# Decay sums and key scales spread by DMA from rows in memory in place of one spreading product per chunk

## The chip, the cores and the metric

The kernel runs on one core of a Trainium2 chip. The metric is the device time of one execution in microseconds (us), the median of the runs.

## The reference, cut to what matters

The model is two blocks, one after the other, on 256 tokens of width 1024. The first block has a gated delta rule beside a sparse attention and an MLP; the second has two layers with a dense and an eight-expert feed-forward part. The change lies in the delta rule. Of each head (8) and chunk, with `g` the log decays and `beta` the gates:

```python
    gc = jnp.cumsum(g, axis=-1)
    decay = jnp.exp(jnp.where(tri_incl, gc[..., :, None] - gc[..., None, :], -jnp.inf))
    kb = k * beta[..., None]
    A = jnp.where(tri_strict, jnp.einsum('bhncd,bhnsd->bhncs', kb, k) * decay, 0.0)
    ...
    w = jnp.einsum('bhncs,bhnsd->bhncd', Tm, kb * jnp.exp(gc)[..., None])
    attn = jnp.einsum('bhncd,bhnsd->bhncs', q, k) * decay
    q_dec = q * jnp.exp(gc)[..., None]
```

`k` and `q` are first scaled to length one, so a token's key carries a factor 1/length. The kernel uses chunks of 128 tokens, so with eight heads there are 16 matrices `m` of 128 by 128 (head `m // 2`, half `m % 2` of the 256 tokens), and a 17th that packs the 16 leading tokens of all eight heads.

## The kernel before

One program for each engine, written out in a fixed order; each waits on named events (semaphores). `q.wait_ge(...)` waits, `.then_inc(*q.did(...))` gives an event. SP only issues DMAs: `sp_blocks` walks a list of weight blocks of 1 MB (eight k-tiles by 256 columns) through a ring of six slots and waits before each until TensorE has used the block that was in its slot; between blocks it issues the other transfers at places named in `sp`. The blocks of the first stage are gk 0 to 3, gq 0 to 3, gv 0 to 3, gz 0 to 3. Each block is cast to a high half by ScalarE (`act_high`, L410) and a low half by VectorE (`dve_low`, L425), and TensorE makes three products of the halves for every tile (`mm3`, L435 to L437). A projected tile goes through a convolution: one tap on ScalarE (L901), three on VectorE (L923), then Silu on ScalarE (L910), then GpSimd squares it (L931) and TensorE sums the squares (L944).

PSUM has eight banks that `Banks.take` hands out in turn; whoever takes a bank waits until its last reader is done.

Beside this run the matrices of the delta rule. `gG` holds the log decays, a column for each matrix; `gB` the gates. `pe_gate_sums` makes the cumulative sums `GC` along the partitions (a column for each matrix). `pe_decays` makes the same sums along the columns, alike on all 128 partitions: a product for each matrix whose stationary operand is the column of `gG` broadcast to 128 columns. `act_factors` (L856) takes the exponential of that in groups of four matrices (it multiplies the queries later). `dve_decays` (L869) subtracts `GC` and cuts off at 0, `act_decays` (L861) takes the exponential in place, and `pool_decays` (L876, L878) multiplies with the two triangular masks into `AT` and `dec`. The five groups are 0 to 3, 4 to 7, 8 to 11, 12 to 15 and 16. ScalarE goes on with `act_l2`, the square root of the keys' lengths (L953); VectorE inverts it (L823) and makes `gBr`, gate over length. `pe_betas` spreads `gBr` over the partitions in the same way, and `dve_betas` (L890) multiplies it into `AT`; then `dve_keys` (L988, L992) takes the key products in, while ScalarE scales the keys (L983). The decays stand in the order of all engines behind block gq 0, the betas of groups 0 and 1 behind gq 2, of 2 and 3 behind gq 3, of the last behind gv 0. When all is in, VectorE inverts the small diagonal blocks (L1200) and spreads them (L1214), and TensorE turns them (L1221) and starts the large inverse. L1703 and L1374 belong to later work, L3500 stores the output, and L3469 reads two rows of gains over all partitions.

Of the kernel before, what the change touches and what calls it, by code (L numbers as in the profile page):

```python
# [15 lines left out]
P = 128  # L16
# [250 lines left out]
def emit(A, cst, out, sem, counts, off, arena, arena_r, ring, ring_r, hi_ring, C, vec, sm, posi, ix, flag, bank):  # L267
# [235 lines left out]
    wr = shaped(small(64), (8, 8))  # L503
    dtb, alog = small(8), small(8)
    eps6, eps5, one1, idle1 = small(1), small(1), small(1), small(1)
    bwr = shaped(sm[:, smtop[0]:smtop[0] + 64], (8, 8))
# [25 lines left out]
    smallT = at(23040, T)  # L532
    wsm, wsmall = at(6400, 8, 24), pair_at(6592, 8, 24)
    l2sq = [at(19456 + SEQ * j, SEQ) for j in range(8)]
    metasq = at(21504, P)
# [183 lines left out]
    def pool_load(q):  # L719
        q.e.memset(ss, 1.0).then_inc(*q.did())  # L720
        for ap, v in ((eps6, 1e-6), (eps5, 1e-5), (one1, 1.0)):
            q.e.memset(ap, v).then_inc(*q.did(("eps",)))
        q.wait_ge(("hi", "half", 1))
        q.e.tensor_tensor(first_half(1, ring_r), first_half(1, ring), first_half(1, hi_ring).bitcast(F32), ALU.subtract).then_inc(*q.did(("lo", "half", 1)))
        q.mark("load")
# [119 lines left out]

    def pe_decays(q, g):
        q.wait_ge(("gG",), ("gB",))
        ps = B.take(q, "decay", g[0])
        for x, m in enumerate(g):
            t = q.e.matmul(ps[:, x * P:(x + 1) * P], gG[:, m:m + 1].to_broadcast([P, P]), cc("Ub" if m == 16 else "U"), start=True, stop=True)  # L850
        t.then_inc(*q.did(("ps", "decay", g[0])))

    def act_factors(q, g):
        q.wait_ge(("ps", "decay", g[0]))
        q.wait_all("load")
        q.e.activation(flat(ebs[g[0] // 4]), B("decay", g[0]), ACT.Exp).then_inc(*q.did(("eb", g[0])))  # L856

# [5 lines left out]
    def dve_decays(q, g):  # L863
        ps = B("decay", g[0])
        q.wait_ge(("ps", "decay", g[0]), ("GC",))
        if g[0] != 16:
            q.wait_ge(("eb", g[0]))
        for x, m in enumerate(g):
            q.e.tensor_scalar(dec[:, m, :], ps[:, x * P:(x + 1) * P], GC[:, m:m + 1], 0.0, ALU.subtract, ALU.min).then_inc(*q.did(("dec0", g[0])))  # L869
        B.drop(("decay", g[0]), ("dec0", g[0]))  # L870

# [7 lines left out]

    def pe_betas(q, g):  # L880
        q.wait_ge(("gBr",))
        ps = B.take(q, "beta", g[0])
        for x, m in enumerate(g):
            t = q.e.matmul(ps[:, x * P:(x + 1) * P], gBr[:, m:m + 1].to_broadcast([P, P]), ident, start=True, stop=True)
        t.then_inc(*q.did(("ps", "beta", g[0])))

    def dve_betas(q, g):
        n = len(g) * P
        q.wait_ge(("ps", "beta", g[0]), ("AT0", g[0]))
        q.e.tensor_tensor(fl(AT, g), fl(AT, g), B("beta", g[0])[:, 0:n], ALU.mult).then_inc(*q.did(("AT1", g[0])))  # L890
        B.drop(("beta", g[0]), ("AT1", g[0]))

# [109 lines left out]
    def act_values(q, g):  # L1002
        q.wait_ge(("ps", "vT", g[0]), ("gB",))
        for x, m in enumerate(g):
            q.e.activation(vb[:, m, :], B("vT", g[0])[:, x * P:(x + 1) * P], ACT.Copy, scale=gB[:, m:m + 1]).then_inc(*q.did(("vb", g[0])))
        B.drop(("vT", g[0]), ("vb", g[0]))
# [25 lines left out]
    def pe_delta_in(q):  # L1032
        for i in range(1, 4):
            for j in pe_tiles(q, "gk", i, "gk", nX, 0, T, xn):
                if j == 2:
                    pe_gate_rows(q)
                if j == 6:
                    pe_gate_meta(q)
            if i >= 2:
                pe_l2(q, "gk", i - 2)  # L1040
        for i in range(4):
            for j in pe_tiles(q, "gq", i, "gq", nX, 0, T, xn):
                if j == 0:
                    pe_gate_sums(q)
            if i == 0:
                for g in groups:
                    pe_decays(q, g)
                pe_l2(q, "gk", 2)
            if i == 1:
                pe_l2(q, "gk", 3)  # L1050
            if i == 2:
                B.full("l2", "gk")
                for g in groups[0:2]:
                    pe_betas(q, g)
                    pe_keys(q, g)
                pe_l2(q, "gq", 0)
            if i == 3:
                pe_l2(q, "gq", 1)
                for g in groups[2:4]:
                    pe_betas(q, g)  # L1060
                    pe_keys(q, g)
        for i in range(4):
# [3 lines left out]
            if i == 0:  # L1066
                pe_betas(q, groups[4])
                pe_keys(q, groups[4])
# [7 lines left out]
    def act_delta_in(q):  # L1076
        for i in range(4):
            if i == 1:
                act_high(q, W.at["gk", 1] + 2)
                act_gate_rows(q)  # L1080
            act_channels(q, "gk", i)
        act_silu(q, "gk", 7)
        act_high(q, W.at["gq", 0] + 2)
        act_gate_sums(q)
        for i in range(4):
            act_channels(q, "gq", i)
            if i == 0:
# [2544 lines left out]
    def sp(e):  # L3632
        q = Engine(e, "sp", counts, sem)
        sp_first(q)
        for i in sp_blocks(q, W):
            if i == 2:
                sp_smalls(q)
            elif i == NRAW - 1:
                sp_consts(q)
# [56 lines left out]
```

## Time and profile before

| | |
|---|---|
| time, median of 3 runs | 1814.17 us (1813.74 to 1815.82) |
| profiled execution: time, span | 1815.71 us, 1814.0 us |
| busy in the span: TensorE, VectorE, ScalarE, GpSimd | 1790.4, 1394.8, 1075.1, 122.6 us |
| moved by DMA | 438.91 MB, 242 GB/s in the mean |

The busy times are sums over one profiled execution. The stage of the change lies between 36 and 143 us of the span. In the rows below PE is TensorE, DVE VectorE, ACT ScalarE, POOL GpSimd and SPq the queue of SP; times are counted from the start of the span. A number in brackets with an arrow is the idle time of the engine before the instruction and what ended it.

### The profile page before, as it was taken

The page shows a single profiled execution, that of the slowest core. Times are in us where ns is not written, and L with a number is a line of the kernel's source. Part 1 is how long each engine was busy: PE and PEld are TensorE (multiplying, and loading weights), DVE is VectorE, ACT ScalarE, POOL GpSimd, SP SyncE. Part 2 cuts the span into 40 slices and gives each one's busy share as a digit, 9 for nine tenths or more (in the row PEclk, how much of TensorE's full clock was granted, in tenths as well). Part 3 has the DMA queues.
Part 4 walks back from the last instruction along what each step waited for, and adds up shares of the span by engine and source line. Part 5 has one row for each costly group of instructions (what it writes and reads, how often), then busy time and mean ns, then how long its engine had stood idle before and what let it go on. Part 6 is the DMA issues. An engine that isn't in the chain of part 4 may idle for free.

```text
span 1814.0 us, 26895 instructions
## 1 busy us (share of the span) xinstructions
PE 1790.4 (99%) x11464; PEld 1611.7 (89%) x11464; DVE 1394.8 (77%) x1643; ACT 1075.1 (59%) x1198; POOL 122.6 (7%) x138
## 2 busy tenths in 40 slices
PE   9999999999999999999999999999999999999997
PEld 8999999999988999998998888888888888888885
DVE  6896487567674566655677899888889898889897
ACT  7753444556544444444336777767777776767674
POOL 1453150000000100000010000000000000000000
PEclk9999999999999999999999999999999999999999
DMA  9341333556555545565453599989998999899993
GB/s 287 116 129 48 94 117 117 181 183 217 186 187 198 186 151 185 185 231 168 152 173 118 202 379 373 369 315 374 352 376 309 377 349 378 308 379 349 378 368 134
DMA packets 260039, 438.91 MB, mean 242 GB/s; under 512 B 10341, under 2 KB 132792, under 8 KB 259784
## 3 DMA queue, kind: packets, MB, share of 16 engines
q1 hardware_dynamic: 259912, 437.11, 69.3%
q8 instruction: 92, 1.51, 0.3%
q14 instruction: 35, 0.29, 0.0%
HBM read 436.04 MB, written 1.05 MB: 241 GB/s over the span
## 4 chain that ended last, share of the span: by engine, by line
PE 90%; DVE 7%; ACT 2%; issue 1%; DMA 0%; SPq 0%; DVEq 0%; ACTq 0%
PE bank L437 26%; PE bank L435 26%; PE bank L436 26%; DVE ring_r L425 2%; PE bank L3208 1%; ACT hi_ring L410 1%; PE bank L3125 1%; PE bank L2488 1%; PE bank L1352 1%; PE bank L1344 1%; DVE arena L923 1%; PE bank L1811 1%; DVE arena L1714 0%; PE bank L1586 0%; DVE arena L1200 0%
## 5 line engine op out<-in xcount | busy, mean ns | idle before, releaser
L425 DVE TENSOR_TENSOR ring_r<-ring,hi_ring 128x2048 fp32r<-128x2048 f32 x402 | 906.9, 2282 | 248.3 <-ACT hi_ring L410 248.2
L410 ACT CAST hi_ring<-ring 128x2048 fp32r<-128x2048 f32 (+1 forms) x404 | 757.5, 1903 | 140.9 <-PE bank L437 140.6
L435 PE MATMUL bank<-hi_ring,arena_r 128*128 128x512 f32 (+1 forms) x1526 | 569.0, 373 | 0.7 <-DVE ring_r L425 0.7
L436 PE MATMUL bank<-ring_r,arena_r 128*128 128x512 f32 (+2 forms) x1534 | 567.4, 370 | 0.0
L437 PE MATMUL bank<-hi_ring,arena_r 128*128 128x512 f32 (+1 forms) x1526 | 566.4, 371 | 0.0
L435 PE MATMUL bank<-ring_r,hi_ring 128*128 128x256 f32 (+1 forms) x1400 | 400.1, 286 | 0.0
L437 PE MATMUL bank<-ring_r 128*128 128x256 f32 (+1 forms) x1400 | 395.4, 282 | 0.0
L436 PE MATMUL bank<-ring_r,hi_ring 128*128 128x256 f32 (+1 forms) x1400 | 395.3, 282 | 0.0
L435 PEld LDWEIGHTS bank<-hi_ring,arena_r 128*128 128x128 f32 x1526 | 286.8, 188 | 52.4 <-DVE ring_r L425 2.4
L436 PEld LDWEIGHTS bank<-ring_r,arena_r 128*128 128x128 f32 (+1 forms) x1534 | 287.9, 188 | 51.1
L437 PEld LDWEIGHTS bank<-hi_ring,arena_r 128*128 128x128 f32 x1526 | 286.9, 188 | 50.4
L435 PEld LDWEIGHTS bank<-ring_r,hi_ring 128*128 128x128 f32 x1400 | 264.6, 189 | 1.8 <-issue 1.0
L437 PEld LDWEIGHTS bank<-ring_r 128*128 128x128 f32 x1400 | 264.7, 189 | 0.0
L436 PEld LDWEIGHTS bank<-ring_r,hi_ring 128*128 128x128 f32 x1400 | 263.8, 188 | 0.2
L498 ACT CAST arena_r<-arena 128x256 fp32r<-128x256 f32 (+1 forms) x84 | 36.2, 434 | 80.1 <-DVE arena L2706 37.6
L498 ACT CAST arena_r<-bank 128x512 fp32r<-128x512 f32 (+1 forms) x62 | 32.3, 526 | 71.6 <-PE bank L3208 67.3
L3247 ACT ACTIVATE arena<-bank 128x512 f32<-128x512 f32 (+1 forms) x48 | 27.1, 564 | 64.6 <-PE bank L437 64.6
L494 DVE TENSOR_TENSOR arena_r<-arena,arena_r 128x256 fp32r<-128x256 f32 (+2 forms) x92 | 46.2, 507 | 3.2 <-ACT arena_r L498 2.2
L1653 ACT ACTIVATE arena<-bank 128x256 f32<-128x256 f32 (+1 forms) x27 | 10.4, 386 | 57.1 <-PE bank L437 57.1
L435 PE MATMUL bank<-arena_r,hi_ring 128*128 128x256 f32 x144 | 40.8, 283 | 0.0
L437 PE MATMUL bank<-arena_r,ring_r 128*128 128x256 f32 x144 | 40.7, 283 | 0.0
L436 PE MATMUL bank<-arena_r,hi_ring 128*128 128x256 f32 x144 | 40.4, 281 | 0.0
(422 smaller groups left out, 1641.8 us busy)
## 6 DMA issues: line engine op xcount, KB each, us to landing
ring<-in_w_gu_moe SPq DMA_DIRECT2D x176, 1024.0 KB, 6.3
ring<-in_w_down_moe SPq DMA_DIRECT2D x88, 1024.0 KB, 5.4
ring<-in_w_in SPq DMA_DIRECT2D x31, 1024.0 KB, 5.3
ring<-in_w_gu_dense SPq DMA_DIRECT2D x22, 1024.0 KB, 5.2
ring<-in_w_up SPq DMA_DIRECT2D x16, 1024.0 KB, 5.5
ring<-in_w_down SPq DMA_DIRECT2D x16, 1024.0 KB, 5.1
ring<-in_w_in_a SPq DMA_DIRECT2D x10, 1024.0 KB, 5.9
ring<-in_w_down_dense SPq DMA_DIRECT2D x10, 1024.0 KB, 5.1
```

The lines of the kernel that those rows point to most:

```text
L410: q.e.copy(hi_ring[:, b:b + m], ring[:, a:a + m]).then_inc(*q.did(("hi", of.tag, i)))
L425: q.e.tensor_tensor(ring_r[:, a:a + m], ring[:, a:a + m], hi_ring[:, b:b + m].bitcast(F32), ALU.subtract).then_inc(*q.did(("lo", of.tag, i)))
L435: q.e.matmul(ps, a[0], b[0], start=first, stop=False)
L436: q.e.matmul(ps, a[0], b[1], start=False, stop=False)
L437: return q.e.matmul(ps, a[1], b[0], start=False, stop=last)
L494: q.e.tensor_tensor(lo, src, hi.bitcast(F32), ALU.subtract).then_inc(*q.did(*done))
L498: q.e.copy(hi, src).then_inc(*q.did(*done))
L923: q.e.scalar_tensor_tensor(out=d, in0=ps[:, 0:T - u], scalar=vcol("conv_w", 24 * (3 - u) + w0 + j), in1=d, op0=ALU.mult, op1=ALU.add).then ...
L1344: t = q.e.matmul(ps[:, x * P:(x + 1) * P], MTs[i % 3][:, x, :], D[:, m, :], start=True, stop=True)
L1352: t = q.e.matmul(ps[:, x * P:(x + 1) * P], Ys[i % 3][:, x, :], DT[:, m, :], start=True, stop=True)
L1811: t = q.e.matmul(ps[p0:p0 + hd, qt * P:(qt + 1) * P], u["v"](j), pt[:, j, :], start=(x == 0), stop=(x == len(use) - 1))
L3247: q.e.activation(hh[:, c0:c0 + n], R.banks(R.tag, "up", x, j, 0)[:, 0:n], ACT.Silu).then_inc(*q.did(("hsilu", R.tag, x, j)))
```

## The change

The sums are made once as 17 rows: `pe_decay_rows` makes a product with `gG` as the stationary operand for 16 matrices and another for the 17th, ScalarE copies both from PSUM to SBUF, SP writes them to a new tensor `rows` in device memory and reads them back with a broadcast over all 128 partitions, group by group, into `dec`. `pe_beta_rows` transposes `gBr` in the middle of gq 2, and the same way leads into `betas`, which lies in the memory of `vb`. `act_factors` and `dve_decays` now read `dec` in SBUF; the latter is a `scalar_tensor_tensor` with a zero column, broadcast, as second input. `act_values`, which writes `vb`, waits for the group's `AT1`. The 34 spreading products and their ten bank turns are gone.

```diff
+    zero1 = small(1)
...
+    cumT, cum16T, betaT, betas = at(23400, P)[0:16, :], at(23528, P)[0:1, :], at(23656, P)[0:17, :], vb
...
-        for ap, v in ((eps6, 1e-6), (eps5, 1e-5), (one1, 1.0)):
+        for ap, v in ((zero1, 0.0), (eps6, 1e-6), (eps5, 1e-5), (one1, 1.0)):
...
-    def pe_decays(q, g):
-        q.wait_ge(("gG",), ("gB",))
-        ps = B.take(q, "decay", g[0])
-        for x, m in enumerate(g):
-            t = q.e.matmul(ps[:, x * P:(x + 1) * P], gG[:, m:m + 1].to_broadcast([P, P]), cc("Ub" if m == 16 else "U"), start=True, stop=True)
-        t.then_inc(*q.did(("ps", "decay", g[0])))
+    def row_of(a):
+        return a.rearrange("a (o b) -> o (a b)", o=1).to_broadcast([P, a.shape[0] * P])
+
+    def pe_decay_rows(q):
+        q.wait_ge(("gG",))
+        ps = B.take(q, "cumT")
+        q.e.matmul(ps[0:16, 0:P], gG[:, 0:16], cc("U"), start=True, stop=True)
+        q.e.matmul(ps[0:1, P:2 * P], gG[:, 16:17], cc("Ub"), start=True, stop=True).then_inc(*q.did(("ps", "cumT")))
+
+    def act_decay_rows(q):
+        q.wait_ge(("ps", "cumT"))
+        q.e.copy(cumT, B("cumT")[0:16, 0:P]).then_inc(*q.did())
+        q.e.copy(cum16T, B("cumT")[0:1, P:2 * P]).then_inc(*q.did(("cumT",)))
+        B.drop(("cumT",), ("cumT",))
+
+    def sp_decays(q):
+
+        q.wait_ge(("cumT",), ("end", "load", "pe"))
+        q.e.dma_start(A["rows"][0:16, :], cumT).then_inc(*q.landed("out_decay"))
+        q.e.dma_start(A["rows"][16:17, :], cum16T).then_inc(*q.landed("out_decay", ("out", "decay")))
+        q.wait_ge(("out", "decay"))
+        for g in groups:
+            q.e.dma_start(fl(dec, g), row_of(A["rows"][g[0]:g[-1] + 1, :])).then_inc(*q.landed(f"in_decay{g[0]}", ("in", "decay", g[0])))
 
     def act_factors(q, g):
-        q.wait_ge(("ps", "decay", g[0]))
+        q.wait_ge(("in", "decay", g[0]))
         q.wait_all("load")
-        q.e.activation(flat(ebs[g[0] // 4]), B("decay", g[0]), ACT.Exp).then_inc(*q.did(("eb", g[0])))
+        q.e.activation(flat(ebs[g[0] // 4]), fl(dec, g), ACT.Exp).then_inc(*q.did(("eb", g[0])))
...
     def dve_decays(q, g):
-        ps = B("decay", g[0])
-        q.wait_ge(("ps", "decay", g[0]), ("GC",))
+        q.wait_ge(("in", "decay", g[0]), ("GC",), ("eps",))
         if g[0] != 16:
             q.wait_ge(("eb", g[0]))
-        for x, m in enumerate(g):
-            q.e.tensor_scalar(dec[:, m, :], ps[:, x * P:(x + 1) * P], GC[:, m:m + 1], 0.0, ALU.subtract, ALU.min).then_inc(*q.did(("dec0", g[0])))
-        B.drop(("decay", g[0]), ("dec0", g[0]))
+        for m in g:
+            q.e.scalar_tensor_tensor(out=dec[:, m, :], in0=dec[:, m, :], scalar=GC[:, m:m + 1], in1=zero1.to_broadcast([P, P]), op0=ALU.subtract, op1=ALU.min).then_inc(*q.did(("dec0", g[0])))
...
-    def pe_betas(q, g):
+    def pe_beta_rows(q):
         q.wait_ge(("gBr",))
-        ps = B.take(q, "beta", g[0])
-        for x, m in enumerate(g):
-            t = q.e.matmul(ps[:, x * P:(x + 1) * P], gBr[:, m:m + 1].to_broadcast([P, P]), ident, start=True, stop=True)
-        t.then_inc(*q.did(("ps", "beta", g[0])))
+        ps = B.take(q, "betaT")
+        q.e.transpose(ps[0:17, 0:P], gBr, ident).then_inc(*q.did(("ps", "betaT")))
+
+    def act_beta_rows(q):
+        q.wait_ge(("ps", "betaT"))
+        q.e.copy(betaT, B("betaT")[0:17, 0:P]).then_inc(*q.did(("betaT",)))
+        B.drop(("betaT",), ("betaT",))
+
+    def sp_betas(q):
+
+        q.wait_ge(("betaT",))
+        q.e.dma_start(A["rows"][32:49, :], betaT).then_inc(*q.landed("out_beta", ("out", "beta")))
+        q.wait_ge(("out", "beta"))
+        for g in groups:
+            q.e.dma_start(fl(betas, g), row_of(A["rows"][32 + g[0]:33 + g[-1], :])).then_inc(*q.landed(f"in_beta{g[0]}", ("in", "beta", g[0])))
 
     def dve_betas(q, g):
-        n = len(g) * P
-        q.wait_ge(("ps", "beta", g[0]), ("AT0", g[0]))
-        q.e.tensor_tensor(fl(AT, g), fl(AT, g), B("beta", g[0])[:, 0:n], ALU.mult).then_inc(*q.did(("AT1", g[0])))
-        B.drop(("beta", g[0]), ("AT1", g[0]))
+        q.wait_ge(("in", "beta", g[0]), ("AT0", g[0]))
+        q.e.tensor_tensor(fl(AT, g), fl(AT, g), fl(betas, g), ALU.mult).then_inc(*q.did(("AT1", g[0])))
...
     def act_values(q, g):
-        q.wait_ge(("ps", "vT", g[0]), ("gB",))
+        q.wait_ge(("ps", "vT", g[0]), ("gB",), ("AT1", g[0]))
...
+            if i == 3:
+                pe_decay_rows(q)
             if i >= 2:
                 pe_l2(q, "gk", i - 2)
         for i in range(4):
             for j in pe_tiles(q, "gq", i, "gq", nX, 0, T, xn):
                 if j == 0:
                     pe_gate_sums(q)
+                if j == 4:
+                    pe_beta_rows(q)
             if i == 0:
-                for g in groups:
-                    pe_decays(q, g)
                 pe_l2(q, "gk", 2)
...
                 for g in groups[0:2]:
-                    pe_betas(q, g)
                     pe_keys(q, g)
...
             act_channels(q, "gk", i)
+        act_decay_rows(q)
         act_silu(q, "gk", 7)
...
         for i in range(4):
+            if i == 2:
+                act_beta_rows(q)
             act_channels(q, "gq", i)
...
+            elif i == W.at["gk", 3] + NRAW:
+                sp_decays(q)
+            elif i == W.at["gq", 1] + NRAW:
+                sp_betas(q)
```

The calls of `pe_betas` for groups 2, 3 and 4 go in the same way.

## Rows read from the trace of the kernel before

**Rows 1.** Busy time of each engine by stage; columns in its first line.
```profile
core 0: us, PE busy (x) PEld busy (x) DVE busy (x) ACT busy (x) POOL busy (x), PEclk, DMA share, GB/s
66.00:79.00 13.00, 13.00 (x109) 12.84 (x108) 12.44 (x30) 9.70 (x19) 8.20 (x9) 1.00 0.37 116
79.00:100.00 21.00, 21.00 (x177) 21.00 (x176) 20.02 (x43) 9.67 (x21) 6.02 (x6) 1.00 0.33 101
```

**Rows 2.** The chain that ended last: start us, us, what.
```profile
51.97 3.79 PE bank L850 x34
...
78.45 1.13 DVE arena L988 x4
...
142.50 1.26 PE bank L1221 x8
```

**Rows 3.** Timeline of VectorE: start us, us, engine, line, operation.
```profile
57.16 2.16 DVE L869 TENSOR_SCALAR arena<-bank,sm 128x128 f32<-128x128 f32 x8 [1.01 <-ACT arena L856]
59.55 2.42 DVE L869 TENSOR_SCALAR arena<-bank,sm 128x128 f32<-128x128 f32 x9 [0.23 <-ACT arena L856]
65.98 0.26 DVE L823 RECIPROCAL sm<-sm 128x17 f32<-128x17 f32 x1 [4.02 <-ACT sm L953]
...
74.69 0.68 DVE L890 TENSOR_TENSOR arena<-arena,bank 128x512 f32<-128x512 f32 x1
...
77.67 0.67 DVE L890 TENSOR_TENSOR arena<-arena,bank 128x512 f32<-128x512 f32 x1
```

**Rows 4.** Timeline of ScalarE, same columns.
```profile
48.64 0.43 ACT L910 ACTIVATE arena<-arena 128x272 f32<-128x272 f32 x1 [1.04 <-DVE arena L923]
...
56.45 1.09 ACT L856 ACTIVATE arena<-bank 128x512 f32<-128x512 f32 x2
...
62.48 1.88 ACT L410 CAST hi_ring<-ring 128x2048 fp32r<-128x2048 f32 x1
...
70.38 0.43 ACT L910 ACTIVATE arena<-arena 128x272 f32<-128x272 f32 x1 [1.93 <-DVE arena L923]
```

**Rows 5.** One line's instructions, L884: ns min/median/max.
```profile
L884 PE MATMUL bank<-consts,sm x34: 272/275/356, 69.7 to 93.7; 128*128 128x128 f32 x34
```

**Rows 6.** DMA issues (page), then lines L3500 (a store) and L3469 (a broadcast read).
```profile
ring<-in_w_in SPq DMA_DIRECT2D x31, 1024.0 KB, 5.3
...
L3500 SPq DMA_DIRECT2D out<-arena x4: 332/338/347, 1807.8 to 1811.3; - x4
...
DMA to landing us min/median/max: 2.0/2.3/2.7
...
L3469 SPq DMA_DIRECT2D arena<-in_vectors x2: 350/389/428, 1782.8 to 1783.2; - x2
...
DMA to landing us min/median/max: 3.5/4.2/5.0
```

**Rows 7.** GpSimd: line L876 as a whole, then its timeline.
```profile
L876 POOL TENSOR_TENSOR arena<-arena,consts x5: 469/1286/1305, 59.0 to 78.2; 128x512 f32<-128x512 f32 x4, 128x128 f32<-128x128 f32 x1
...
75.54 1.29 POOL L876 TENSOR_TENSOR arena<-arena,consts 128x512 f32<-128x512 f32 x1
...
80.21 0.61 POOL L931 TENSOR_TENSOR arena<-arena 128x256 f32<-128x256 f32 x1 [0.46 <-ACT arena L910]
...
86.47 2.13 POOL L931 TENSOR_TENSOR arena<-arena 128x256 f32<-128x256 f32 x1 [0.86 <-ACT arena L910]
```

**Rows 8.** Pairs of VectorE and GpSimd: timelines, then groups by line and form.
```profile
122.30 3.80 POOL L1374 TENSOR_TENSOR arena<-arena,consts 128x512 f32<-128x512 f32 x3 [1.76 <-PE bank L999]
...
123.85 1.03 DVE L1200 TENSOR_TENSOR arena<-arena 128x12 f32<-128x12 f32 x1
...
126.67 0.21 DVE L1200 TENSOR_TENSOR arena<-arena 128x30 f32<-128x30 f32 x1
...
L425 DVE TENSOR_TENSOR ring_r<-ring,hi_ring 128x2048 fp32r<-128x2048 f32 x399 | 903.2, 2290 | 237.1 <-ACT hi_ring L410 237.1
...
L1703 DVE SCALAR_TENSOR_TENSOR arena<-arena,sm 128x272 f32<-128x272 f32 x7 | 3.5, 502 | 3.4 <-ACT arena L1662 2.8
...
L1703 DVE SCALAR_TENSOR_TENSOR arena<-arena,sm 128x144 f32<-128x144 f32 x7 | 3.1, 440 | 0.7
```

More of the change, by code:

```diff
@@ L1059, in pe_delta_in @@
                 for g in groups[2:4]:
-                    pe_betas(q, g)
                     pe_keys(q, g)
@@ L1066, in pe_delta_in @@
             if i == 0:
-                pe_betas(q, groups[4])
                 pe_keys(q, groups[4])
@@ L3691 @@
     cst = nc.dram_tensor("in_table", table.shape, F32, kind="ExternalInput").ap()
+    aps["rows"] = nc.dram_tensor("rows", (64, P), F32).ap()
     out = nc.dram_tensor("out_0", (1, SEQ, 1024), F32, kind="ExternalOutput").ap()
```

## The prediction

> **What bounds the kernel now.** I read the page for the whole, then only the stretch that the change touches, 36 to 143 us: busy time by stage, the waits, the chain, and each engine's timeline. Every stage behind it starts on what this one delivers, so a shift at 142.5 us arrives at the end.
>
> In busy time by stage [rows 1] TensorE is full in every stretch, but so, nearly, is VectorE from 66 us on (12.44 of 13.00, 20.02 of 21.00). The chain [rows 2] runs through TensorE up to 78.45 us, the 3.79 us of the decay products among it, then through VectorE, and TensorE comes back into it only at 142.50, when VectorE releases it. I don't follow the chain before 78 us. VectorE's timeline [rows 3] has no gap at 78.45, its key product there simply follows on the beta product of 77.67. Its last real idle time is the 4.02 us that end at 65.98, and what ended it is ScalarE's square root [rows 3]. ScalarE in turn [rows 4] works without a break through the exponentials of the decays, the cast at 62.48, a table load behind it and the root. Those exponentials alternate with VectorE's 17 subtractions (57.16 to 61.97). So the path is: ScalarE and VectorE on the decays, cast, table load, root, then VectorE alone for 76 us. TensorE runs ahead of it and never holds it. TensorE's own slack at the end of the stretch is small (it waits a little before 142.50), but everything the change takes from TensorE adds to that slack.
>
> **The change, part by part.**
>
> TensorE. The 17 decay products are 34 passes of 3.79 us in all [rows 2]; the 17 beta products are 34 passes of the same kind (median 275 ns each, started about 0.11 us apart as 3.79/34) [rows 5], so 3.8 us. Added are two products (4 passes) and one transpose (1 or 2): 0.6 us. Net 7.0 us less. Worth 0 on the path, since VectorE from 66 us and ScalarE before it don't wait for these products. What hides TensorE's loss hides its gain as well. A new wait comes with it: the beta transpose stands inside the product of gq tiles 4 and 5, and needs gBr, which VectorE makes right behind 65.98. TensorE, 3.3 us early by then, waits there until about 66.6. That gives back what the decays saved; tile 5 is then done at about the time of before, and nobody waits for it.
>
> Decay rows: are they there in time? ScalarE copies the sums in the idle time before the activation of 48.64 (1.04 us idle) [rows 4], two copies of about 0.2 us; ready at 48.1. SP sends them out (two DMAs, 0.4 us apart), behind a weight block that is issued when gk 3 is done, at about 44, and lands in some 5.3 us [rows 6], so by 49.5. A store of 256 KB lands in 2.0 to 2.7 us [rows 6]: out at about 51.1. A broadcast read of 512 KB over the 128 partitions lands in 3.5 us when it is first [rows 6], the 256 KB store in 2.3; I take 2.8 for a group of 256 KB: first group at 53.9, the others about 0.7 us apart, the last at 56.8. Needed: first at 56.45, the last of the four behind 59.5. Worth 0, with 2.5 us of cover. Were the landing 5 us, it would be a stall of 1 to 2 us. Behind it in SP's queue stand weight blocks that come 1.5 us late, with six blocks loaded ahead: 0.
>
> Decay subtraction. Before: tensor_scalar with its input in PSUM, 17 in two runs of 2.16 and 2.42 us, 0.26 us apart [rows 3]. After: scalar_tensor_tensor with the broadcast rows in SBUF and a broadcast zero in SBUF. By itself it costs the same 0.26. But now it has two inputs in SBUF, and GpSimd's mask products of 1.29 us, two for each group, start at 59.0 [rows 7]; four in a row reach to 64.3, beside the second half of the subtractions. What the trace shows of such pairs [rows 8]: while GpSimd does its three products of 122.30 to 126.10, a VectorE product of 12 columns out of SBUF takes 1.03 us, ending as GpSimd's instruction ends; with GpSimd idle one of 30 columns takes 0.21. The scalar_tensor_tensor L1703 with 144 columns averages 440 ns against 502 for 272 columns; 128 columns fewer, at the 1.12 ns each of the low halves (2290 ns over 2048 columns), should leave 360, so some of the seven were held too. The other way, GpSimd's 0.61 us square took 2.13 us beside VectorE's subtraction for a low half (L425), at 86.47 [rows 7]. The PSUM forms at 59.55 ran beside GpSimd's product undisturbed [rows 3, 7].
>
> The Trainium skill says the same and more widely, on the page "SBUF — State Buffer", section "Who interferes with whom": a VectorE instruction with two SBUF inputs contends with a GpSimd instruction that reads SBUF, and whoever starts first holds the shared pair for the whole instruction. It counts inputs, not columns, so by it the one-column zero would count as the second input, a case that no row shows; by it the sum below stands, and without it (a one-column input taken as none) this term would be 0.
>
> Worked out: groups 0 and 1 (8 subtractions) are over at 59.3, before GpSimd holds anything. Group 2 starts at 59.55. GpSimd has five instructions before it next waits for ScalarE: four of 1.25 us and one of 0.6. VectorE gets one subtraction in behind each: 60.5, 61.9, 63.2, 64.6 (group 2 done), 65.4, then freely 65.6, 65.9, 66.1 (group 3) and 66.4. Before, the last ended at 61.97. ScalarE's last exponential, cast, load and root follow: +4.4 us at VectorE's 65.98. Bounds: 0 if a one-column input takes no port; at least 0.9 if VectorE waits only once (59.55 to 60.45); at most 5.3 if all 5.6 us of GpSimd's work lies ahead of VectorE's nine.
>
> Betas: late. All times here without the shift just found, which moves both sides alike. ScalarE copies the rows behind the activation of 70.38 [rows 4]: ready at 71.0. Out 2.0 to 2.7 [rows 6], issue and wait 0.05, back 2.3 to 3.5: the first group is there between 75.35 and 77.25, at my 2.3 and 2.8 at 76.15. VectorE wants it at 74.69 [rows 3]: a stall of 0.7 to 2.6, taken as 1.5 us, with all of VectorE's queue behind it (keys, the next low half, the convolutions of gq 3). Nothing hides it: group 0's mask product, the other input, is done by 60.4, and the beta products used to stand in PSUM by then. The later groups come in time.
>
> Beta products: 0.68 us for 512 columns out of PSUM and SBUF [rows 3]; out of SBUF alone 0.57 by the 1.12 ns a column of the low halves, and a start, so I take the same. But they too now have two SBUF inputs, and GpSimd's masks of groups 2 to 4 run up to about 79 [rows 7]. At 76.2 the instruction of 75.54 still has 0.6 us to go; the second product meets a short one, 0.3; the third the square of 86.47 that ends at 88.6, 0.5. Together 1.4 us; bounds 0 and 2.5 (two long ones whole).
>
> Sum on the path: 0 (TensorE) + 4.4 + 1.5 + 1.4 = 7.3 us. The profiled execution's span is 1814.0 and its time 1815.7, 1.5 us above the median of the three runs, 1814.17; a shift carries over to that median: 1821.5 us.
>
> **The rivals.** (1) TensorE is the bound after all, as the chain before 78 us says: then 7.0 us less, 1807.2. It decides if VectorE, in truth, follows TensorE's tiles between 66 and 142 us; against it stands that VectorE's busy time leaves under 1 us in 21 [rows 1], and that its waits name ScalarE [rows 3]. (2) The one-column zero takes no port; only the late betas and their port cost: 1.5 + 1.4 = 2.9 us, or 0.7 with the early landing and no collision: 1814.9 to 1817.1, no change that can be measured (a measurement of this kernel can tell about 0.2%, 3.6 us). (3) A transfer takes 5 us or more from issue to landing, as blocks do: decays 1 to 2 us late and betas 4 more, on top of the sum: 1825 and above. (4) Everything lands in time and nothing collides, 1814.
>
> **How the numbers follow.** Forecast (port and late betas) 0.60; rival (2) 0.18; (4) 0.07; (1) 0.08; (3) 0.07. The low bound of the first case is 0.9 + 0.7 = 1.6 us, its high bound 5.3 + 2.6 + 2.5 = 10.4 us. The range 1814 to 1825 holds the first two cases and most of (4); out are (1) and (3). Slower by over 0.2%: the first case but for its lowest part, and (3): 0.65. Within: 0.25. Faster: 0.10.
>
> **What would show it.** Right: VectorE's subtractions of groups 2 and 3 take over 1 us each with their ends on the ends of GpSimd's masks, the root comes near 70.4, the first beta product starts behind its DMA's landing, TensorE idles in front of the beta transpose, and TensorE's restart of 142.50 comes 7 us later. Wrong: subtractions that keep 0.26 us apart (then rival 2), a beta product without a wait, or a restart before 142.5 (rival 1).

## The result, and the profile after

The changed kernel takes 1823.64 us (1820.93 to 1824.82, 5 runs) against 1814.17 us (1813.74 to 1815.82, 5 runs): a ratio of 1.0045 by all the runs (the two medians alone would give 1.0052), 95% interval 1.0035 to 1.0056. The interval does not hold 1, so the changed kernel is slower, by about half a percent. The profiled execution of it took 1823.64 us, with a span of 1821.7 us, 7.7 us over the span of before.

Read first busy time by stage, beside [rows 1]:

```profile
core 0: us, PE busy (x) PEld busy (x) DVE busy (x) ACT busy (x) POOL busy (x), PEclk, DMA share, GB/s
66.00:79.00 13.00, 8.42 (x52) 8.42 (x53) 8.51 (x18) 9.88 (x16) 4.30 (x5) 0.62 0.10 22
79.00:100.00 21.00, 18.84 (x154) 18.45 (x153) 19.50 (x43) 11.15 (x26) 9.49 (x10) 1.00 0.59 191
```

From 66 to 79 us TensorE and VectorE both lost more than 3 us of work: TensorE stands idle, and its granted clock over the stretch is 0.62 of full speed, so much of it is spent at the lower level, 1.2 GHz. The DMA queues are nearly still (0.10 against 0.37). Something in front of this stretch is late. VectorE's timeline names it, beside [rows 3] (the single rows from 59.32 on come from narrow windows; they are the first five of the nine subtractions):

```profile
56.90 2.19 DVE L887 SCALAR_TENSOR_TENSOR arena<-arena,sm 128x128 f32<-128x128 f32 x8 [1.04 <-ACT arena L875]
59.32 6.72 DVE L887 SCALAR_TENSOR_TENSOR arena<-arena,sm 128x128 f32<-128x128 f32 x9 [0.23 <-ACT arena L875]
...
59.32 1.04 DVE L887 SCALAR_TENSOR_TENSOR arena<-arena,sm 128x128 f32<-128x128 f32 x1 [0.23 <-ACT arena L875]
60.29 1.44 DVE L887 SCALAR_TENSOR_TENSOR arena<-arena,sm 128x128 f32<-128x128 f32 x1
61.65 1.38 DVE L887 SCALAR_TENSOR_TENSOR arena<-arena,sm 128x128 f32<-128x128 f32 x1
62.95 1.42 DVE L887 SCALAR_TENSOR_TENSOR arena<-arena,sm 128x128 f32<-128x128 f32 x1
64.30 0.70 DVE L887 SCALAR_TENSOR_TENSOR arena<-arena,sm 128x128 f32<-128x128 f32 x1
...
70.05 0.26 DVE L825 RECIPROCAL sm<-sm 128x17 f32<-128x17 f32 x1 [4.01 <-ACT sm L979]
...
79.95 1.48 DVE L917 TENSOR_TENSOR arena<-arena 128x512 f32<-128x512 f32 x1 [1.11 <-DMA arena<-rows]
...
83.60 1.06 DVE L917 TENSOR_TENSOR arena<-arena 128x512 f32<-128x512 f32 x1
...
94.19 1.10 DVE L917 TENSOR_TENSOR arena<-arena 128x512 f32<-128x512 f32 x1
...
105.49 0.28 DVE L917 TENSOR_TENSOR arena<-arena 128x128 f32<-128x128 f32 x1
```

GpSimd's timeline beside it:

```profile
58.78 1.44 POOL L893 TENSOR_TENSOR arena<-arena,consts 128x512 f32<-128x512 f32 x1 [8.37 <-ACT arena L880]
60.30 1.29 POOL L895 TENSOR_TENSOR arena<-arena,consts 128x512 f32<-128x512 f32 x1
61.54 1.34 POOL L893 TENSOR_TENSOR arena<-arena,consts 128x512 f32<-128x512 f32 x1
62.96 1.27 POOL L895 TENSOR_TENSOR arena<-arena,consts 128x512 f32<-128x512 f32 x1
64.19 0.66 POOL L957 TENSOR_TENSOR arena<-arena 128x256 f32<-128x256 f32 x1
```

The first eight subtractions follow each other at 0.26 us, as before. Of the nine, five take 1.04, 1.44, 1.38, 1.42 and 0.70 us, and each ends within 0.2 us of the end of one of GpSimd's five instructions (60.22, 61.59, 62.88, 64.23, 64.85). Behind 64.85 the last four pass in 1.1 us. ScalarE waits for them, beside [rows 4], and SP's queue carries the betas' round trip, beside [rows 6]:

```profile
64.41 0.63 ACT L880 ACTIVATE arena<-arena 128x512 f32<-128x512 f32 x1 [4.14 <-DVE arena L887]
...
66.55 1.88 ACT L410 CAST hi_ring<-ring 128x2048 fp32r<-128x2048 f32 x1
...
74.78 0.24 ACT L904 COPY arena<-bank 17x128 f32<-17x128 f32 x1
```

```profile
50.97 2.24 SPq L870 DMA_DIRECT2D arena<-rows  x5
...
75.05 0.25 SPq L910 DMA_DIRECT2D rows<-arena  x1
76.59 2.24 SPq L913 DMA_DIRECT2D arena<-rows  x5
```

The chain that ended last, beside [rows 2], passes through both transfers, as it never did before:

```profile
61.65 4.14 DVE arena L887 x6
...
75.05 1.53 DMA rows<-arena
76.59 3.33 DMA arena<-rows
79.95 1.49 DVE arena L917
...
149.88 1.26 PE bank L1249 x8
```

TensorE's wait list has the expected new entry, `PEld bank L900 <- DVE sm L827: 7.3, 1, 7.3`: one wait of 7.3 us before the beta transpose. It restarts on the diagonal blocks, which it turns, at 149.88 instead of 142.50 [rows 2], 7.4 us later. This restart is called the restart below.

### The profile page after: what moved, and what is told of

Same layout as the page of the kernel before. It is cut to its first block, busy times and chain, and to the rows that moved or that the text cites. A ratio compares the mean times of both kernels' runs of the same rounds, so it can differ in the third digit from the quotient of the medians.

```text
span 1821.7 us, 26786 instructions
## 1 busy us (share of the span) xinstructions
PE 1789.5 (98%) x11401; PEld 1610.9 (88%) x11401; DVE 1400.7 (77%) x1643; ACT 1075.4 (59%) x1201; POOL 120.4 (7%) x139
## 4 chain that ended last, share of the span: by engine, by line
PE 88%; DVE 8%; ACT 3%; issue 1%; DMA 1%; SPq 0%; DVEq 0%; ACTq 0%
PE bank L437 26%; PE bank L435 26%; PE bank L436 26%; DVE ring_r L425 2%; DVE arena L949 1%; ACT hi_ring L410 1%; PE bank L3236 1%; PE bank L3153 1%; PE bank L2516 1%; PE bank L1380 1%; PE bank L1372 1%; PE bank L1614 1%; PE bank L1839 1%; DVE arena L1228 0%; PE bank L3360 0%
```

## The experiments

The delay is built up in four segments of one path, and each run is read by them (a beta product is VectorE's multiplication of the betas into `AT` for one group): from the first subtraction to the reciprocal, from there to the start of the first beta product, from there to the start of the last, and from there to TensorE's restart. In the kernel before they are 8.82, 8.71, 24.22 and 43.59 us: 57.16, 65.98, 74.69 and 142.50 [rows 2, 3], with

```profile
98.91 0.28 DVE L890 TENSOR_TENSOR arena<-arena,bank 128x128 f32<-128x128 f32 x1
```

The table gives what each kernel's single profiled execution adds to them, in us, and the ratio of all its runs (5 to 11) to those of the kernel before beside it (24 to 28 runs, median 1815.3 to 1815.7; for the first row the 5 runs given above, median 1814.17). The sum leaves out when the first subtraction starts: at 56.6 to 57.6 us in most executions, at 59.0 in that of masks_as_before and at 55.9 in the last two rows.

| kernel | subtractions to reciprocal | to first beta product | to last | to restart | sum | median | ratio (95%) |
|---|---|---|---|---|---|---|---|
| the change | 4.33 | 1.19 | 1.32 | 0.80 | 7.64 | 1823.64 | 1.0045 (1.0035-1.0056) |
| change_again | 4.33 | 1.08 | 1.46 | 0 | 6.86 | 1821.09 | 1.0034 (1.0021-1.0048) |
| decays_only | 4.38 | 0 | 0 | 0 | 4.35 | 1819.63 | 1.0023 (1.0013-1.0033) |
| scales_only | 0 | 1.02 | 1.52 | 0 | 2.53 | 1819.14 | 1.0018 (1.0009-1.0027) |
| zero_in_psum | 0 | 0.98 | 1.53 | -0.1 | 2.40 | 1816.83 | 1.0010 (1.0001-1.0019) |
| masks_wait | 0.08 | 2.55 | 1.37 | 0.4 | 4.44 | 1819.97 | 1.0023 (1.0012-1.0033) |
| filler | 4.36 | 1.14 | 1.41 | 0 | 6.94 | 1821.17 | 1.0034 (1.0021-1.0048) |
| copy_early | 4.33 | 0 | 1.11 | 0.5 | 5.94 | 1821.88 | 1.0032 (1.0020-1.0045) |
| repaired | 0 | 1.47 | 0.41 | 1.0 | 2.95 | 1817.99 | 1.0014 (1.0005-1.0023) |
| gpsimd_scales | 0 | 1.46 | -1.7 for both | | -0.20 | 1814.51 | 0.9995 (0.9986-1.0004) |
| masks_as_before | 0 | 0 | 0.2 for both | | 0.18 | 1816.22 | 1.0003 (0.9994-1.0012) |
| silu_later | 0 | 1.45 | -2.4 for both | | -0.87 | 1814.29 | 0.9994 (0.9985-1.0003) |
| before_silu_later | 0 | 0 | 0.3 for both | | 0.26 | 1815.35 | 1.0000 (0.9991-1.0009) |

**The change again (change_again).** The same kernel, timed beside the next three.

> The changed kernel once more, on the chip of the three runs beside it. The path's own delay in its profile is 7.4 us (TensorE's restart at 149.88 against 142.50), the medians are 9.5 us apart. If the 2 us between the two are only the spread of the executions of both kernels, this run lies 7 to 9 us above the kernel before; if they belong to the change (say, a lower clock of TensorE later on), 9 to 10 us again.

Slower again, by 5.8 us in the medians, which is less than the 7 to 9 us expected. The first three segments repeat to 0.15 us; the 0.80 us in the last one do not. They lay in VectorE's inversion, where in the first profile a 128-column product took 1.24 us beside GpSimd, and 0.29 in this one. Of the runs below four show nothing in that segment and three show 0.4 to 1.0 us: in copy_early the same product takes 1.24 us again, in masks_wait and repaired a product of 4 columns takes 1.09 and 1.19 instead of 0.66 in the kernel before. I take it for a chance of where GpSimd's three products of 1.3 us fall there; no run was made to show it.

**One half alone (decays_only, scales_only).** In the first the betas are spread by TensorE again, in the second the decays:

```diff
 # decays_only
-        q.e.tensor_tensor(fl(AT, g), fl(AT, g), fl(betas, g), ALU.mult)
+        q.e.tensor_tensor(fl(AT, g), fl(AT, g), B("beta", g[0])[:, 0:n], ALU.mult)
 # scales_only
-            q.e.scalar_tensor_tensor(out=dec[:, m, :], in0=dec[:, m, :], scalar=GC[:, m:m + 1], in1=zero1.to_broadcast([P, P]), ...)
+            q.e.tensor_scalar(dec[:, m, :], ps[:, x * P:(x + 1) * P], GC[:, m:m + 1], 0.0, ...)
```

> Only the decay sums go by way of memory; the key scales are spread by TensorE as before. Theory (second SBUF input of VectorE's subtraction collides with GpSimd's masks): the root comes at 69.8 as in the change, plus 4.1 us in all, 4 to 5 us above the kernel before. Rival A (the late key scales are the real cost and the subtractions' delay is swallowed later): within 1 us of the kernel before. Rival B (TensorE's idle time in front of the beta transpose lowers its clock and that costs): under 4 us, since that idle time is gone.

> Only the key scales go by way of memory; the decay sums are spread by TensorE as before, into PSUM. Theory: VectorE's subtractions keep 0.26 us apart and the root stays at 65.7; the first product of the scales waits about 1.2 us for its DMA, and three of the products take 0.4 to 0.8 us longer beside GpSimd: 2.5 to 3.5 us above the kernel before. Rival A (late scales are the real cost): 6 us or more.

The two parts add up: 4.35 and 2.53 make 6.88, and the whole has 6.86. VectorE's timeline of decays_only, then that of scales_only:

```profile
59.02 6.77 DVE L887 SCALAR_TENSOR_TENSOR arena<-arena,sm 128x128 f32<-128x128 f32 x9 [0.23 <-ACT arena L875]
...
78.50 0.68 DVE L925 TENSOR_TENSOR arena<-arena,bank 128x512 f32<-128x512 f32 x1
```

```profile
59.16 2.42 DVE L895 TENSOR_SCALAR arena<-bank,sm 128x128 f32<-128x128 f32 x9 [0.22 <-ACT arena L882]
...
75.33 1.67 DVE L926 TENSOR_TENSOR arena<-arena 128x512 f32<-128x512 f32 x1 [0.94 <-DMA arena<-rows]
```

The stretched subtractions come with the decays' half alone, the wait for the transfer and the long beta products with the betas' half alone. The time of scales_only, 3.9 us over the kernel before in the medians, is more than its 2.5 us on the path and more than the 3.5 expected. What the clock does to a time (below) is as large as the rest: the profiled execution, at a mean granted clock of 0.996, took 1816.53 us, the four at 0.993 took 1819.1 to 1820.6.

**The zero moved to PSUM (zero_in_psum).** The instruction, its counts and its first input stay; only the one column that holds the zero lies in a free column of a PSUM bank.

```diff
+        zp = B("cumT")[:, 256:257]
+        if g[0] == 0:
+            q.e.memset(zp, 0.0).then_inc(*q.did(("zp",)))
-   in1=zero1.to_broadcast([P, P])
+   in1=zp.to_broadcast([P, P])
```

> The whole change, but the zero column of the subtraction lies in PSUM, so that it has one SBUF input. Theory: the 17 subtractions are 0.26 us apart again, ScalarE's root comes near 65.7 in place of 69.7, and the time falls by 4 to 4.5 us against the change (some 3 to 4 us above the kernel before). Rival (the form scalar_tensor_tensor in place on DMA-written rows is slow, or ScalarE waits for the DMAs): no change against the changed kernel.

```profile
59.46 2.42 DVE L892 SCALAR_TENSOR_TENSOR arena<-arena,sm,bank 128x128 f32<-128x128 f32 x9 [0.25 <-ACT arena L875]
65.91 0.26 DVE L825 RECIPROCAL sm<-sm 128x17 f32<-128x17 f32 x1 [4.02 <-ACT sm L984]
...
75.59 1.71 DVE L922 TENSOR_TENSOR arena<-arena 128x512 f32<-128x512 f32 x1 [0.90 <-DMA arena<-rows]
```

6.72 us become 2.42, with GpSimd's masks of 58.92 to 64.2 us beside them as before. So a second input of one column, repeated for all 128, is enough for the collision when it lies in SBUF, and the whole first segment was this. What is left of the change, 2.40 us, is that of scales_only. The median, 1816.83 us, is 4.3 us under that of change_again, as expected, but only 1.5 us over the kernel before, where 3 to 4 were expected.

**GpSimd made to wait (masks_wait).** The zero is in SBUF again, but GpSimd starts its masks only when all subtractions are done (`if g[0] == 0: q.wait_ge(("dec0", 16))` in `pool_decays`).

> The whole change, and one wait more: GpSimd holds its first mask product until VectorE's 17th subtraction is done. Nothing else is touched; both SBUF inputs stay. Theory (the subtractions are slow only beside GpSimd's reads): they are 0.26 us apart, the last ends near 61.8, the root comes near 65.8, GpSimd starts some 3 us later, which nobody on the path notices: 4 to 4.5 us less than the change, 1 to 3 us above the kernel before. Rival (form, in-place access or the DMA-written rows make them slow): the subtractions stay at 1.3 us each and the added wait makes it slower by up to 3 us.

VectorE's timeline, and under it GpSimd's:

```profile
59.67 2.45 DVE L887 SCALAR_TENSOR_TENSOR arena<-arena,sm 128x128 f32<-128x128 f32 x9 [0.23 <-ACT arena L875]
66.14 0.26 DVE L825 RECIPROCAL sm<-sm 128x17 f32<-128x17 f32 x1 [4.02 <-ACT sm L981]
66.44 1.08 DVE L827 TENSOR_TENSOR sm<-sm 128x17 f32<-128x17 f32 x1
...
67.55 0.56 DVE L831 SCALAR_TENSOR_TENSOR sm<-sm 128x17 f32<-128x17 f32 x1
...
77.40 1.43 DVE L919 TENSOR_TENSOR arena<-arena 128x512 f32<-128x512 f32 x1 [1.18 <-DMA arena<-rows]
```

```profile
62.27 1.31 POOL L895 TENSOR_TENSOR arena<-arena,consts 128x512 f32<-128x512 f32 x1 [11.52 <-DVE arena L887]
...
66.23 1.26 POOL L897 TENSOR_TENSOR arena<-arena,consts 128x512 f32<-128x512 f32 x1
```

With GpSimd out of the way the subtractions are 0.26 us apart with both inputs in SBUF, so it is the pairing that costs and not the instruction. But the masks now lie 3.5 us later, beside the 17-column products L827 and L831 (0.18 us each otherwise), which are held for 1.08 and 0.56 us. That makes everything behind late by 1.3 us, the betas' rows with it, and the wait for them is still there: 4.3 us won, 1.5 of them given back. The expectation, that nobody on the path would notice GpSimd's late start, was wrong, and the median is 1.1 us under that of change_again instead of 4 to 4.5.

**TensorE kept busy (filler).** 30 products of the identity, written to unused columns, fill TensorE's wait in front of the beta transpose.

> The whole change, and 30 products of the identity with itself (60 passes, about 6.6 us) in TensorE's idle time in front of the beta transpose. If the lowered clock of TensorE behind that idle time (0.62 in the stage 66 to 79 us) costs time, this is 1 to 2 us faster than the change and its granted clock stays at full speed there. If TensorE has slack there, the time is that of the change within 1 us, at 5.5 to 6.5 us above the kernel before.

Windows 66 to 79 us of change_again, then of filler:

```profile
66.00:79.00 13.00, 8.27 (x60) 8.27 (x61) 8.67 (x18) 9.82 (x16) 4.14 (x5) 0.74 0.08 20
```

```profile
66.00:79.00 13.00, 12.51 (x107) 12.24 (x106) 8.68 (x19) 9.78 (x16) 4.06 (x5) 1.00 0.04 15
```

The granted clock rises from 0.74 to 1.00, and the restart stays (6.94 against 6.86 us). The idle TensorE and its low clock in this stretch cost nothing; they are a sign of the delay and not its cause.

**The betas' rows copied earlier (copy_early).** ScalarE's copy out of PSUM moves from the end of block gq 1, behind the tap of tile 3, to the middle of that block, behind the tap of tile 2.

```diff
+            if (name, j) == ("gq", 2):
+                act_beta_rows(q)
...
-            if i == 2:
-                act_beta_rows(q)
```

> The changed kernel with one thing moved: ScalarE copies the betas' rows out of PSUM right behind its tap and SiLU beside the third channel row of gq, where it had done so some us later, so their round trip through memory starts earlier. Theory (lateness and port add up): the first beta product no longer waits for its transfer (1.1 us in the changed kernel, and some 0.15 more for VectorE's issue), the subtractions stay at 6.7 us and the beta products at 1.1 to 1.6 us; restart of TensorE's chain at 148 to 149, time 1 us under the changed kernel, 1820 to 1822.5. Rival (the wait for the transfer is the whole cost of the beta part): the restart falls by 2.5 us or more. Rival (the copy then holds ScalarE's SiLU, which was due first): the restart doesn't move or goes up.

On the path it did as forecast: from the reciprocal to the first beta product it is 8.71 us again, without a wait, and the second segment's 1.1 us are gone. The time does not show it: 1821.88 against 1821.09 us for the change. The clock alone moves a time by more than 1 us from one execution to the next (below), so 1 us cannot be told here from the times, only from the path.

**What would repair it (repaired, gpsimd_scales, masks_as_before).** The first has the zero in PSUM, the early copy, and GpSimd's masks of all five groups before its squares of gq, so that the later beta products meet no mask. The second lets GpSimd do the beta products of groups 1 to 4 itself, in front of its squares of gq from tile 4 on. The third is the second with the old order of masks and squares. The diff is cut to GpSimd's order in the first two; its last two lines are not in repaired.

```diff
-        for g in groups[0:2]:
+        for g in groups:
             pool_decays(q, g)
         pool_l2(q, "gq", range(0, 4))
-        for g in groups[2:5]:
-            pool_decays(q, g)
...
+        for g in groups[1:5]:
+            pool_betas(q, g)
```

> The whole change with all three costs taken out: zero column in PSUM; ScalarE's copy of the key scales moved ahead by two tiles' work (from behind gq tile 3 to behind gq tile 2), so that they land before VectorE wants them; GpSimd's masks all ahead of its squares of the queries, so that none runs beside the products of the scales. Theory: root near 65.9, first product of the scales without a wait near 74.6 at 0.7 us, TensorE's restart near 142.5, the time within 1 us of the kernel before: the 7 us taken from TensorE are still worth nothing. Rival (TensorE's work counts once the waits are gone): 1 to 7 us faster than the kernel before.

> As repaired, and the products of the scales of groups 1 to 4 go from VectorE to GpSimd, which can read them now that they lie in SBUF (it cannot take part while they are in PSUM in this kernel's order). Theory (VectorE is the path from 66 to 142 us): it saves VectorE 3 times 0.78 and once 0.76 us, restart near 139.5 to 140.5, 2 to 3 us faster than the kernel before. Rival (the products then come late, or GpSimd's reads hold VectorE up by as much): within 1 us of repaired.

> The version with the zero in PSUM, the early copy of the betas' rows and GpSimd doing the last four beta products, but with GpSimd's masks and squares in the order of the changed kernel (masks of the first two groups, squares of gq, masks of the other three). If the two small VectorE operations beside the masks (0.59 and 1.23 us in that version, 0.18 for the second in the kernel before) are what costs it, this one restarts TensorE's chain 1 to 1.5 us earlier, at 141 to 141.6 where that version had 142.6, and takes 1813 to 1814.5. If the masks of the last groups are then late for the key products and the beta products that follow, the restart is at 143 or later and the time 1815 or more.

repaired was expected to be back within 1 us of the kernel before. It is 2.95 us late on the path and 2.6 us in the medians. Its timeline of VectorE:

```profile
66.42 0.59 DVE L827 TENSOR_TENSOR sm<-sm 128x17 f32<-128x17 f32 x1
66.93 0.16 DVE L829 TENSOR_TENSOR sm<-sm 128x17 f32<-128x17 f32 x1
67.04 1.23 DVE L831 SCALAR_TENSOR_TENSOR sm<-sm 128x17 f32<-128x17 f32 x1
...
76.29 0.68 DVE L922 TENSOR_TENSOR arena<-arena 128x512 f32<-128x512 f32 x1
```

The first beta product is free of wait and collision (0.68 us). But GpSimd's run of masks now stretches over the small products, which cost 1.46 us more. Moving the masks moved the collision. gpsimd_scales has the same 1.46 us and takes four of the five beta products off VectorE; the one left to VectorE takes 1.62 us instead of 0.68, now beside GpSimd's own beta products (four in 4.67 us from 75.00). It comes out level with the kernel before (ratio 0.9995), not 2 to 3 us faster as expected. In masks_as_before the small products are at 0.18 us again, as its expectation had it, but the time is not better. Its restart, at 144.53, proves less than it seems to: this execution was 1.8 us late before its first subtraction (59.00 against 57.16), and by the segments it is only 0.2 us behind the kernel before. VectorE, then GpSimd:

```profile
79.19 1.11 DVE L1031 TENSOR_SCALAR arena<-bank,sm 128x128 f32<-128x128 f32 x4
82.85 1.13 DVE L1027 SCALAR_TENSOR_TENSOR arena<-bank,sm,arena 128x128 f32<-128x128 f32 x4 [2.55 <-PE bank L1012]
```

```profile
80.52 0.46 POOL L898 TENSOR_TENSOR arena<-arena,consts 128x128 f32<-128x128 f32 x1
81.06 0.46 POOL L900 TENSOR_TENSOR arena<-arena,consts 128x128 f32<-128x128 f32 x1
81.48 6.19 POOL L922 TENSOR_TENSOR arena<-arena 128x512 f32<-128x512 f32 x4
```

The wait of 2.55 us names TensorE, whose products for that group had been done since before 74. What it really waits for is the other input: GpSimd's first beta product starts at 81.48, behind six masks, and its end lies where the wait ends. That is the rival of the expectation, masks late for the beta products. gpsimd_scales has no such wait, and what was won at the small products is lost again here.

**ScalarE's order (silu_later, before_silu_later).** On gpsimd_scales, and on the kernel before, the Silu of gq's first tile moves behind the root, which saves two table loads of 1.28 us.

> The version with the zero in PSUM, the early copy and GpSimd doing the last four beta products, with one more edit: ScalarE's SiLU of gq's first channel row waits until the root is done, so that ScalarE loads its function tables two times fewer between 55 and 80 us. If those loads (about 1.3 us each in the timeline) stand on the path to the first beta product, the restart is 1 to 2.6 us earlier and the time 1812 to 1813.5; if ScalarE has slack there, nothing moves (1814 to 1815).

> The kernel before with that one edit to ScalarE's order alone (the SiLU of gq's first channel row behind the root). If the table loads stand on the path, it gains as much here as on the other version, 1 to 2.6 us (1812 to 1814); if the gain there needs the other edits, this one is within 0.5 us of the kernel before.

In both the first subtraction comes earlier (55.9 instead of 57.2 to 57.5), so the loads did stand on the path, but only about half of them: VectorE now goes from its convolutions into the first subtraction without idle time, so 55.9 is as early as its own work allows. In silu_later ScalarE waits 2.0 us for the decays' rows, so the cover that the first transfer had is used up, though for the same reason that wait costs nothing yet. Its restart is at 140.35, 2.1 us before that of the kernel before, the earliest of all; before_silu_later has 141.52. The times don't prove a gain: medians 1814.29 and 1815.35 us, both above what was expected of a gain, ratios 0.9994 and 1.0000, both intervals holding 1. No version that beats both kernels beyond the measurement was found.

## Why the prediction was right

The time forecast was 1821.5 us; it is 1823.64 in the first runs and 1821.09 in the second. That both lie so near is in part luck, as the last point below tells; the path is what bears the forecast out. By its steps:

- **TensorE, 7.0 us less work, worth 0.** Right. It waited 7.3 us in front of the transpose (forecast: 3.3, plus the 4.4 of the delay), and filler, which gives TensorE that work back in the wait and holds its clock, restarts at the same time: neither the work nor the wait nor its clock costs or gains anything. Rival 1 is out.
- **Decay rows in time.** Right. SP issued the write at 47.6 and the read at 50.97, against 51.1 in the forecast; the first group landed 3.3 us later, at 54.3, against 53.9, and ScalarE took it at 56.16. The write took 3.3 us to its waiter, more than the 2.0 to 2.7 of the rows that I had gone by. The cover was 1.9 us (forecast 2.5), and silu_later, which wants the rows at 53, waits for them.
- **The subtraction's port.** Forecast +4.4, measured +4.30 in the nine subtractions (6.72 against 2.42), with one let through behind each of GpSimd's five instructions. The question that no row of before could answer was whether one broadcast column counts as an input. zero_in_psum answers it, and with it rival 2 falls. By the rule of the Trainium skill, page "SBUF — State Buffer", section "Who interferes with whom", this is a VectorE instruction with two SBUF inputs beside a GpSimd one that reads SBUF; the traces agree, at 128 columns, at 17 and with a stride of zero.
- **Betas late.** Forecast 1.5 us, measured 1.1 to 1.2. The write and its wait took 1.53 us and the first read 3.33; I had 2.3 and 2.8, two errors that nearly cancel. Rival 3, 5 us from issue to landing, held for the last groups only (4.9 and 5.4 us at most), which nobody wants so early.
- **Beta products.** Forecast 1.4, measured 1.3 to 1.5: 1.48 us for the first instead of 0.68, then 1.06 and 1.10. The fourth met nothing. I had put the first product's share at 0.6 and it was 0.8.
- **What follows unhindered.** The prediction said that VectorE has no idle time behind 65.98. It has two waits for ScalarE's casts, 0.73 us before 108.31 and 0.83 before 115.42; the changed kernel has them too (0.73 and 0.81), so they swallowed nothing of the delay.
- **The sum.** 7.3 us forecast, 6.9 to 7.6 on the path. The medians moved 9.5 and 5.8 us. The 9.5 are counted from five runs of the kernel before with median 1814.17; its 25 runs beside change_again have 1815.29, from which the same 7.3 us would have given 1822.6, between the two results. Profiled execution against profiled execution the spans differ by 7.7 us in the first case and 5.3 in the second. The restart accounts for 7.4 and 6.75 of them, what lies behind it for +0.3 and -1.45, the latter with 3.4 us less at the lower clock (below).

## What to carry to other kernels

An operand moved from PSUM to SBUF changes who the instruction collides with, also when it is a constant of one column: count the SBUF inputs of every VectorE instruction that runs beside GpSimd, put one of them in PSUM where there is room, and expect the smallest products to pay most, since a hold is as long as GpSimd's instruction. Taking work from an engine that runs ahead of the path (34 products of TensorE) bought nothing here; a round trip through memory in its place costs some 5 us of latency, so it wants its start that much ahead of its reader. Moving the neighbour instead of the operand only picks another victim, so look along its new place first.

## What the runs showed of the hardware

Small products are held as long as large ones: 17 columns took 1.08 us (masks_wait) and 1.23 (repaired) instead of 0.18 beside GpSimd's masks of 1.3 us.

The transfers' latency differs with what else is under way: the decays' rows took 3.3 us from the first issue of their write to its waiter, with the DMA engines busy for 0.22 of the time, the betas' rows 1.53 us, with them busy for 0.02. This is one case of each, and the first is two transfers.

The spread of one kernel's times, 1813.7 to 1818.1 us over 28 runs of the kernel before, is of the size of the effects, and much of it goes with the granted clock: the seven runs with a mean of 0.997 took 1813.7 to 1814.8 us, the others, at 0.994 to 0.996, 1815.2 or more. Every profiled execution has a stretch near 235 us at the lower level, though by the busy time TensorE had been at work in all of the 80 us ahead of it (80.00 of 80.00 us between 150 and 230 in the kernel before). In two kernels, before and change_again:

```profile
230.00:250.00 20.00, 20.00 (x144) 18.48 (x141) 14.89 (x48) 10.51 (x19) 7.71 (x6) 0.83 0.35 105
```

```profile
230.00:250.00 20.00, 20.00 (x157) 17.84 (x157) 15.67 (x40) 11.59 (x30) 6.66 (x6) 0.91 0.17 54
```

What TensorE did before its clock fell is the same in all fourteen profiled executions. It had begun on the sums of the heads' squares, 32 products with a single moving column each, which count as busy time; the clock falls between 1.9 and 4.5 us behind their start, at 232.9 in the kernel before, whose timeline of TensorE has

```profile
230.19 4.56 PE L1544 MATMUL bank<-consts,arena 128*128 128x1 f32 x32
```

No run leaves these products out, so that they are the cause is not shown.

A mean of 0.83 over 20 us is 6.8 us at half speed, one of 0.91 is 3.4. From the restart to the end of the span the first has 1671.5 us (1814.0 - 142.5), the second 1670.05 (1819.3 - 149.25). The other twelve fall in line. Four of the fourteen have 3.4 us more at the lower level right behind the restart. Counted over both places, the six executions with 3.4 us take 1669.9 to 1670.3 us from the restart to the end, the seven with 6.8 take 1671.3 to 1671.8, and masks_wait with 10.2 takes 1673.3. So each further 3.4 us at the lower level in these places costs about 1.5 us, and the same kernel can have either: the change had 6.8 us in its first profile and 3.4 in its second. What decides between the two these runs do not say.
